# The first S5 layer's block pipeline: low halves on VectorE from PSUM, power tables read from a PSUM bank, and an earlier table step

## The reference, cut to what matters

```python
def s5_mixer(u, lam_re, lam_im, log_dt, b_re, b_im, c_re, c_im, d, w_glu):
    # 64 groups of 16 channels, 64 complex states each
    dt = jnp.exp(log_dt)[:, None]
    a = exp(lam * dt)                      # a_r, a_i
    bb = (a - 1) / lam * b                 # bb_r, bb_i
    ...
    bu = einsum('gnh,btgh->btgn', bb, u)
    x_t = a * x_{t-1} + bu_t               # associative scan over the tokens
    y = einsum('ghn,btgn->btgh', c_re, xr) - einsum('ghn,btgn->btgh', c_im, xi)
    y = y + d * u
    y = gelu(y)
    ab = y @ w_glu
    return ab[..., :dm] * sigmoid(ab[..., dm:])
```

## Time and profile before

| | before |
|---|---|
| median of 3 runs | 2085.6 us (2083.46 to 2087.68) |
| the profiled execution, its own time | 2085.45 us |
| its span in the trace | 2083.7 us |
| PE busy over the span | 1944.7 us (93%) |
| DVE, ACT, POOL busy | 1279.2, 898.9, 433.5 us |
| granted TensorE clock, mean | 0.973 |

### The profile page before, as it was taken

How to read it: one execution, slowest core, us unless ns; L and a number is a source line. 1 busy time by engine, 2 the same in 40 slices (tenths; PEclk the granted TensorE clock), 3 DMA queues, 4 the chain that set the end, 5 groups by cost and what they waited for, 6 DMA issues and landing times.

```text
span 2083.7 us, 27291 instructions
## 1 busy us (share of the span) xinstructions
PE 1944.7 (93%) x9494; PEld 1564.5 (75%) x9494; DVE 1279.2 (61%) x1783; ACT 898.9 (43%) x1503; POOL 433.5 (21%) x295
## 2 busy tenths in 40 slices
PE   3879999999999967999999999999999998999996
PEld 2668788888887745788888887878878886777774
DVE  7984443433469587543343468987667765777764
ACT  3674432332335255432232333445445552466661
POOL 4772200000044010300000044352212224100003
PEclk7899999999999979999999999999999999999998
DMA  4213333333332200332333332222222222222221
GB/s 178 45 33 108 94 91 101 93 98 99 93 99 84 84 6 11 91 100 91 101 93 99 96 96 81 81 61 63 70 79 64 71 71 62 91 62 62 70 71 61
DMA packets 54522, 166.98 MB, mean 80 GB/s; under 512 B 13216, under 2 KB 13344, under 8 KB 53920
## 3 DMA queue, kind: packets, MB, share of 16 engines
q1 hardware_dynamic: 54432, 165.78, 26.6%
HBM read 161.30 MB, written 2.10 MB: 78 GB/s over the span
## 4 chain that ended last, share of the span: by engine, by line
PE 74%; DVE 12%; ACT 5%; POOL 3%; issue 3%; DMA 2%; DVEq 0%; POOLq 0%; SPq 0%; PEldq 0%
PE bank L183 15%; PE bank L184 15%; PE bank L185 15%; PE bank L1478 3%; PE bank L1479 3%; PE bank L1480 3%; DMA raw<-in_w_dram 2%; PE bank L2084 2%; PE bank L2086 2%; PE bank L2085 2%; PE bank L1493 1%; POOL acc L234 1%; PE bank L1494 1%; PE bank L1495 1%; ACT w_hi L195 1%
## 5 line engine op out<-in xcount | busy, mean ns | idle before, releaser
L203 DVE TENSOR_TENSOR w_lo<-raw,w_hi 128x1024 fp32r<-128x1024 f32 x286 | 367.2, 1284 | 460.8 <-ACT w_hi L195 459.4
L195 ACT ACTIVATE w_hi<-raw 128x1024 fp32r<-128x1024 f32 x289 | 305.8, 1058 | 627.2 <-DMA raw<-in_w_dram 627.2
L183 PE MATMUL bank<-x1h,w_hi 128*128 128x512 f32 x744 | 291.6, 392 | 6.6 <-DVE x1l L218 6.6
L185 PE MATMUL bank<-x1h,w_lo 128*128 128x512 f32 x744 | 289.7, 389 | 0.0
L184 PE MATMUL bank<-x1l,w_hi 128*128 128x512 f32 x744 | 289.7, 389 | 0.0
L183 PE MATMUL bank<-x0h,w_hi 128*128 128x512 f32 x704 | 277.9, 395 | 0.0
L185 PE MATMUL bank<-x0h,w_lo 128*128 128x512 f32 x704 | 274.1, 389 | 0.0
L184 PE MATMUL bank<-x0l,w_hi 128*128 128x512 f32 x704 | 274.0, 389 | 0.0
L232 POOL TENSOR_TENSOR sq<-h 128x512 f32 (+1 forms) x64 | 79.0, 1234 | 784.0 <-DVEq L917 660.4
L183 PEld LDWEIGHTS bank<-x1h,w_hi 128*128 128x128 f32 x744 | 139.7, 188 | 38.1 <-DVE x1l L218 7.9
L184 PEld LDWEIGHTS bank<-x1l,w_hi 128*128 128x128 f32 x744 | 139.8, 188 | 29.3 <-issue 0.7
(11 more groups left out here) (379 smaller groups left out, 3464.7 us busy)
## 6 DMA issues: line engine op xcount, KB each, us to landing
raw<-in_w_dram SPq DMA_DIRECT2D x289, 512.0 KB, 3.5
h<-in_xT_dram SPq DMA_DIRECT2D x1, 2048.0 KB, 12.6
Ur<-in_xu_dram SPq DMA_DIRECT2D x8, 256.0 KB, 2.7
out_dram<-h SPq DMA_DIRECT2D x8, 256.0 KB, 2.2
const<-in_const_dram SPq DMA_DIRECT2D x1, 1028.0 KB, 14.6
B_st<-in_B_dram SPq DMA_DIRECT2D x1, 1024.0 KB, 6.8
C_st<-in_C_dram SPq DMA_DIRECT2D x1, 1024.0 KB, 14.6
p_in<-in_pT_dram SPq DMA_DIRECT2D x1, 1024.0 KB, 5.1
```

The source lines that it names most:

```text
L183: e.matmul(b, w_hi[:, w, k], xh[:, k], start=(k == 0), stop=False)
L185: last = e.matmul(b, w_lo[:, w, k], xh[:, k], start=False, stop=(k == KT - 1))
L195: e.activation(w_hi[:, z], raw[:, z], ACT.Copy).then_inc(hi_split, 1)
L203: e.tensor_tensor(w_lo[:, z], raw[:, z], w_hi[:, z].bitcast(F32), ALU.subtract).then_inc(w_split, 1)
```

## The change

There are five edits, all in the S5 mixer. First, `low` goes from GpSimd to VectorE: ScalarE writes the second GELU back into bank 7 and VectorE subtracts `x1h` from bank 7, behind `W` of the next block, in the same loop step as before (T-2), and the last one in an added step. ScalarE no longer waits for `low` ahead of `g`; TensorE's transposes into bank 7 wait for `low` in place of `g`. Second, ScalarE copies the powers of blocks 1 to 4 into bank 1 (`keep_powers`, two copies ahead of the squares) and those of blocks 5 to 7 at T = 4, and VectorE's `tables` takes the powers from there for every block but the first. Third, to free bank 1 both halves of `TB` are transposed into bank 0, so the second half waits for ScalarE's copy of the first; transposes, direct products and their copies take turns by halves. Fourth, `c_powers(GB, SG)` stands right behind `c_powers(0, GB)`, ahead of the phases and the norm. Fifth, ScalarE opens its counters at its start.

```diff
@@ s5_pool
-            s5_low.open(e)
...
-            def low(q):
-                e.wait_ge(s5_gelu.sem, s5_gelu.at("g", q))
-                s5_low.took("lo", tt(x1l[:, q].rearrange("p (c s) -> p s c", s=STEP), a32[:, :].rearrange("p (s c) -> p s c", s=STEP),
-                                     x1h[:, q].bitcast(F32).rearrange("p (c s) -> p s c", s=STEP), ALU.subtract))
-                e.wait_ge(s5_low.sem, s5_low.at("lo", q))
-                e.sem_inc(x_ready, 1)
...
-                if 0 <= T - 2:
-                    low(T - 2)
@@ s5_scalar
+            for counters in (s5_kept, s5_st_kept, s5_k_kept, s5_angles, s5_y_kept, s5_gelu):
+                counters.open(e)
...
             e.activation(flat(power["cos"]), flat(power["whole"]), ACT.Sin, bias=half_pi[:, :], scale=-SIN_SCALE).then_inc(trig_ready, 1)
+            e.wait_ge(psi_ready, 1)
+            keep_powers(e, 1)
             e.wait_ge(h_loaded, 16)
...
-                    s5_st_kept.took(f"ST{k}", e.activation(ST[:, 4 * k - 4:4 * k, :], bk[k - 1].rearrange("p (g n) -> p g n", g=4), ACT.Copy))
+                    s5_st_kept.took(f"ST{k}", e.activation(ST[:, 4 * k - 4:4 * k, :], bk[0].rearrange("p (g n) -> p g n", g=4), ACT.Copy))
...
+                elif T < NBLK:
+                    for k in (1, 2):
+                        st_kept(T, (k,))
+                        k_kept(T, (k,))
+                    if T == 4:
+                        e.wait_ge(s5_tables.sem, s5_tables.at("TBb", 4))
+                        keep_powers(e, 5)
...
-                    e.wait_ge(s5_low.sem, s5_low.at("lo", q - 1))
-                    s5_gelu.took("g", e.activation(a32[:, :], bk[7], ACT.Gelu_apprx_tanh))
+                    s5_gelu.took("g", e.activation(bk[7], bk[7], ACT.Gelu_apprx_tanh))
...
-            for counters in (s5_kept, s5_st_kept, s5_k_kept, s5_angles, s5_y_kept, s5_gelu):
-                counters.open(e)
...
+        def powers(r, z):
+            return bank[1][:, (4 * r + z) * 64:(4 * r + z) * 64 + 64].rearrange("p (g s) -> p g s", g=GB)
+
+        def keep_powers(e, q0):
+            for r in range(2):
+                n = min(4, NBLK - q0)
+                last = e.activation(bank[1][:, 256 * r:256 * r + 64 * n].rearrange("p (g s) -> p g s", s=STEP), PB[:, r, q0 * GB:(q0 + n) * GB, 0:STEP], ACT.Copy)
+            last.then_inc(powers_kept, 1)
@@ s5_vector
-                s5_tables.took("TB1", tt(TB[:, :, :, :], cut(B_st[:, 0], q).unsqueeze(2).to_broadcast(f4), cut(PB[:, 0], q)[:, :, 0:STEP].unsqueeze(3).to_broadcast(f4), ALU.mult))
+                if q:
+                    e.wait_ge(powers_kept, 1 if q <= 4 else 2)
+                kept = [powers(r, (q - 1) % 4) if q else cut(PB[:, r], q)[:, :, 0:STEP] for r in range(2)]
+                s5_tables.took("TB1", tt(TB[:, :, :, :], cut(B_st[:, 0], q).unsqueeze(2).to_broadcast(f4), kept[0].unsqueeze(3).to_broadcast(f4), ALU.mult))
...
-                    s5_tables.took(f"p{k}", tt(second, B_st[:, 1, g0:g0 + 4].unsqueeze(2).to_broadcast(f), PB[:, 1, g0:g0 + 4, 0:STEP].unsqueeze(3).to_broadcast(f), ALU.mult))
+                    s5_tables.took(f"p{k}", tt(second, B_st[:, 1, g0:g0 + 4].unsqueeze(2).to_broadcast(f), kept[1][:, 4 * k - 4:4 * k].unsqueeze(3).to_broadcast(f), ALU.mult))
...
+            def low(q):
+                e.wait_ge(s5_gelu.sem, s5_gelu.at("g", q))
+                s5_low.took("lo", tt(x1l[:, q].rearrange("p (c s) -> p s c", s=STEP), bk[7].rearrange("p (s c) -> p s c", s=STEP),
+                                     x1h[:, q].bitcast(F32).rearrange("p (c s) -> p s c", s=STEP), ALU.subtract))
+                e.wait_ge(s5_low.sem, s5_low.at("lo", q))
+                e.sem_inc(x_ready, 1)
...
             c_powers(0, GB)
+            c_powers(GB, SG)
...
-            c_powers(GB, SG)
...
+                    if q:
+                        low(q - 1)
...
+                if T == NBLK + 1:
+                    low(T - 2)
@@ s5_tensor
-            def transposed(q):
-                for k in (1, 2):
+            def transposed(q, ks=(1, 2)):
+                for k in ks:
...
-                    e.wait_ge(s5_st_kept.sem, s5_st_kept.at(f"ST{k}", q - 1))
+                    e.wait_ge(s5_st_kept.sem, s5_st_kept.at(f"ST{3 - k}", q - 2 + k))
...
-                        last = e.transpose(bank[k - 1][:, g * LANES:(g + 1) * LANES], TB[:, 4 * k - 4 + g].rearrange("p s h -> p (s h)"), C("ident"))
+                        last = e.transpose(bank[0][:, g * LANES:(g + 1) * LANES], TB[:, 4 * k - 4 + g].rearrange("p s h -> p (s h)"), C("ident"))
...
+                elif T < NBLK:
+                    for k in (1, 2):
+                        transposed(T, (k,))
+                        direct(T, (k,))
...
-                    e.wait_ge(s5_gelu.sem, s5_gelu.at("g", q - 1))
+                    e.wait_ge(s5_low.sem, s5_low.at("lo", q - 1))
```

More of the change, by code:

```diff
@@ L336, in program @@
             sem(n) for n in ("zeroed", "dt_ready", "power_steps", "magnitudes", "trig_ready", "tables_ready", "ru_ready"))
-        psi_ready, g_loaded, b_gained, par_rest, const_rest = (sem(n) for n in ("psi_ready", "g_loaded", "b_gained", "par_rest", "const_rest"))
+        powers_kept, psi_ready, g_loaded, b_gained, par_rest, const_rest = (sem(n) for n in ("powers_kept", "psi_ready", "g_loaded", "b_gained", "par_rest", "const_rest"))
         vec_chain, u_loaded = sem("vec_chain"), sem("u_loaded")
@@ L569, in s5_vector @@
             e.memset(Wb[:, :, 0:1], 0.0).then_inc(zeroed, 1)
-            for counters in (s5_tables, s5_phases, s5_states, s5_direct, s5_inputs):
+            for counters in (s5_tables, s5_phases, s5_low, s5_states, s5_direct, s5_inputs):
                 counters.open(e)
@@ L727, in step @@
                     link(e, tt(between[:, 1], V("final"), V("final"), ALU.mult))
-            for T in range(NBLK + 1):
+            for T in range(NBLK + 2):
                 step(T)
```

26 lines of the change are left out of this document (12 added, 14 removed).

## The result

The changed kernel took 2097.05 us in the median of six runs (2092.66 to 2100.34), the kernel before 2086.52 beside it: ratio 1.0045, 95% interval 1.003 to 1.0061. It is slower, as the likeliest sign said, but by 10.5 us where 4.3 were forecast, and outside the range. On a second chip, with twelve runs, it was 2095.17 against 2087.76 us, ratio 1.0031 (1.0015 to 1.0048).

The account below looks back on a forecast made before the run. VectorE was taken to bound the mixer, with mutual waits between it and GpSimd. Front 1.9 plus loop 2.4 gave 4.3 us on 2085.6, so 2089.9 us; the range ran from below Rival A's 2084.9 to 2093.5 us.

Parts of the forecast that it names:

- the likeliest sign: Whole kernel: slower at 47%, against 45% within about 0.2% (4.2 us) and 8% faster.
- The front: Start of the mixer, up to `tables(1)`: later `Ub` and K of block 0 cost 1.9 us, bounds 0 and 3.5.
- `mag` and phases 1.7, the norm and `Ub` 3.7: VectorE behind `c_powers(GB, SG)` in block 0: these two times in us put the end of `Ub` at about 40.9 us.
- the lock: VectorE instructions with two SBUF operands and GpSimd's instructions wait for each other; an operand in PSUM waits for nobody.
- Rival C: TensorE's clock rises to 2.4 GHz before the first outputs, block 1 is 2 us shorter, 2087.9 us; chance 9%.
- The loop: Five periods from the second to the seventh Z: cost 2.4 us, from 1.9 to 3.1 by the subtraction's length.
- GpSimd's half of the period: In the loop: `po1` waits for the third TC instruction and ends 16.0 us behind Z, before 15.58; periods 13.97 us.
- The end of the mixer: Last blocks: ScalarE and TensorE set the pace, cost nothing; 0.5 to 1 us once if a cover is gone.
- The weight splits: Seventh block: GpSimd's three splits come earlier and catch `po1` for about 1.1 us, hidden under the wait for the cosine.
- Behind the mixer: After the mixer TensorE runs without a pause once `x1h` and `x1l` are there, so the 4.3 us shift stays in full.
- Rival A: In the loop: `po1` comes before GpSimd's third TC instruction starts, periods 12.7 us, kernel 2084.9 us; chance 13%.
- Rival B: In the front: GpSimd's early work falls into VectorE's pauses, `tables(1)` 8 us earlier than now, kernel 2080 us; chance 8%.

Follow-up runs that it names:

- banks_alone: Kernel before with only the powers in bank 1 and transposes in bank 0, transposes and direct products in halves: 2081.88 us, ratio 0.9962.
- warm_end: Changed kernel with eight state sums repeated in TensorE's pause ahead of Z, in block 7 alone: 2089.27 us, ratio 1.001 to the kernel before.
- banks_turn: banks_early with GpSimd's second TC instruction made to wait for `po1` of the block two before: 2073.91 us, ratio 0.9937 to the kernel before.
- banks_early: Changed kernel with `c_powers(GB, SG)` at its old place and the subtraction back on GpSimd: 2076.90 us, ratio 0.9936 to the kernel before.
- turn_taken: Changed kernel with GpSimd's second TC instruction waiting for `po1` of the block two before: 2090.77 us, ratio 1.001 to the kernel before.

## Why the prediction was wrong, point by point

- **The front: mechanism right, size off.** `c_powers(0, GB)` ended at 25.5 us (forecast 26), `c_powers(GB, SG)` at 35.4 (35.5), `tables(1)` took 4.0 us. But `Ub` was over at 43.4, not 40.9. The mis-sized term is "`mag` and phases 1.7, the norm and `Ub` 3.7": it took 3.7 and 4.35 us. I had held `mag` to be free of the lock, since it has one input; it waited for 2 us. (`tables(0)` too is not all "with two SBUF operands", since its adds read a bank; that moved nothing, as `c_powers(0, GB)` shows.) In place of 1.9 the front cost 4.4 us at the first Z.
- **Rival C happened as well, and luck came on top.** The clock rose ahead of the outputs of block 0, and the first distance was 12.26 us instead of 15.20, so 2.9 us shorter. I had priced the clock at -2 us and given it 9%. But 1.8 of the 2.9 us are `po1`, which took 0.70 instead of 2.51 us, because GpSimd had nothing to do at 62 us; this was in no term. The waits for TensorE went from 1.38 to 0.63 us, and 1.1 us at most are left for the clock. In banks_alone, with `po1` still at 2.52 us and the clock at 1.00 from 60 us on, the same distance is 13.47 us, 1.7 less than before. These gains hide most of the front's excess at the second Z.
- **The loop: right sum, by luck; the step on GpSimd's half of the period failed.** The five distances cost 2.6 us, forecast 2.4. One by one they changed by -0.6, +1.7, +0.8, +1.2 and -0.5 us, where I had +0.65 for the first and +0.53 for each of the others (less 0.38 once). By my own terms the bounds of this sum were 1.8 and 3.3, not 1.9 and 3.1. `low` added 1.16 us (1.95 from the start of `W` to that of `TB1` in the rows above, 0.79 without it), forecast 1.0; `TB1` gave back 0.36. `po1`, which I had behind the third TC instruction in four of five blocks, was 0.71, 2.99, 2.13, 2.51 and 1.12 us. It ended behind the third in two blocks only (2.99 and 2.51) and behind the second in two (2.13 and 1.12), since in these two GpSimd's angles did not start 6.08 us behind Z but 8.61 and 7.55. A period is 12.15 us plus `po1`, and the cold sums have a share in where it falls.
- **"The end of the mixer": this step failed.** I put it at nothing. It cost 3.1 us (4.0 at the seventh Z to 7.1 at the end). I looked for work that becomes late and did not ask what TensorE's pauses do to its clock. It fell about the pause of 2.05 us ahead of the turn of Z, and that is the whole of it: from the seventh Z to the end it is 22.3 us before, 25.4 after and 21.9 in warm_end, where the pause is filled. Why the clock outlived a pause of 1.93 us in the kernel before stays open. The weight splits held `po1` of the seventh block for 1.9 us (forecast 1.1), which cost nothing, as forecast.
- **Behind the mixer: right as far as the runs tell.** The shift stays and nothing systematic shows. The marks add up to 4.4 - 2.9 + 2.6 + 3.1 = 7.1 us (rounded); the 10.5 us of the first measurement hold another 3 us of spread.
- **Rival A came half true.** `po1` got ahead of the third TC instruction in three of the five blocks, in two of them by the reason that I had given for it (late angles); but there it waited for the second, and no period was as short as 12.7 us. For the kernels without `low` on VectorE it was true one instruction earlier. I priced the banks by what `TB1` saves (0.35 us a block). They save 1.3 us a block, because the 0.35 us bring `po1` into a pause: it falls from 2.1 to 0.70 us, and 0.45 us of that come back as a wait for the angles. The change gave this away by moving `low`, which puts 1.16 us on VectorE and takes 1.5 us off GpSimd; no run parts the two. **Rival B** did not happen.

## What to carry to other kernels

Where two engines exclude each other, an edit is worth not its own time but what it does to the turn in which they meet: 0.35 us less in front of `po1` won 1.3 us a block, and moving `low` from one of the engines to the other lost it again. If a phase matters, a wait on the engine that has slack can fix it: `po1` was at 0.70 us in every block of banks_turn, and the mixer 4.1 us shorter in the trace, though the ratio can't be told from that of banks_early. In turn_taken the same wait won little, since the clock then set the period. A change that moves another engine's pauses has to be charged with what that engine's clock does in them.

## What the runs showed of the hardware

- A VectorE instruction with one input also waits for GpSimd if input and output lie in SBUF: `mag` (128x64) took 2.19 us behind a TC instruction, and 0.22 us without one in banks_alone; with its output in a bank (line 648, `bank<-R`) it took 0.67 to 0.70 us in every row read. The Trainium skill names the case ("SBUF — State Buffer", "SBUF: two separate sides"): a VectorE operation in a mode that uses two ports takes the shared pair as one with two SBUF inputs does. Rows agree, and my rule lacked that half.
- TensorE's granted clock stayed at 1.00 in the kernel before over pauses of 1.93 us ahead of the turns of Z, and in the changed kernel it fell to 1.2 GHz about pauses of 1.64, 1.97 and 2.05 us (the sums behind them took 3.52 us in the last two). The length of the pause alone doesn't decide it, and a loop can sit close to losing its clock without a sign of it.
- Executions of one kernel spread by up to 18 us, and most of that lies behind the mixer: two profiled executions of the changed kernel had their ends at 169.8 and 169.5 us and took 2100.12 and 2093.08 us. The slower executions have the lower granted clock: of the first six of the changed kernel the three at 2099.6 to 2100.3 us had a mean of 0.967 or 0.968, the three at 2092.7 to 2094.5 us 0.970 or 0.971. What lowers it in one execution and not in the next is not shown.
